# The first stage of a two-block layer kernel: order of the first loads, squares on two engines, and three of eight modulation blocks summed on VectorE

## The reference

```python
def rmsnorm(x, g):
    xf = x.astype(jnp.float32)
    xf = xf * lax.rsqrt(jnp.mean(xf * xf, axis=-1, keepdims=True) + EPS)
    return xf.astype(x.dtype) * g
...
    mod = c_act @ ada_w + ada_b                       # c_act = silu(c), one vector of 1024
    sh1, sc1, gt1, sh2, sc2, gt2 = [m[:, None, :] for m in jnp.split(mod, 6, axis=-1)]
    h = rmsnorm(x, mix_pre_g) * (1.0 + sc1) + sh1
    proj = h @ w_in
```

## Time and profile before

| | us |
|---|---|
| median of 3 runs (1496.1 to 1496.56) | 1496.12 |
| the profiled execution's own time | 1496.44 |
| its span in the trace | 1494.4 |
| PE busy / DVE / ACT / POOL in the span | 1482.8 / 783.5 / 528.4 / 952.2 |

### The profile page before, as it was taken

The page is one execution under the profiler, slowest core; times in us unless marked ns, Lnnn a source line. Parts: engine busy times, 40 slices in busy tenths (PEclk is TensorE's granted clock), DMA queues, the critical chain, the costliest instruction groups (busy, mean ns, idle before and its releaser), DMA issues.

```text
span 1494.4 us, 22386 instructions
## 1 busy us (share of the span) xinstructions
PE 1482.8 (99%) x7834; PEld 1213.3 (81%) x7834; DVE 783.5 (52%) x1088; ACT 528.4 (35%) x943; POOL 952.2 (64%) x945
## 2 busy tenths in 40 slices
PE   8999999999999999999999999999999999999998
PEld 6778877888788888888988888888888778787876
DVE  3556676576566657323755554400474572836533
ACT  4481641361262221112522222200342644645432
POOL 5456657665765789788277777798336564655543
PEclk9999999999999999999999999999999999999999
DMA  9244434533533344635022333344133222222231
GB/s 377 90 129 139 129 107 129 168 109 124 180 107 115 114 143 163 127 105 196 29 84 98 98 98 98 99 134 134 57 130 116 64 83 62 79 70 70 72 126 57
DMA packets 67981, 172.29 MB, mean 115 GB/s; under 512 B 7728, under 2 KB 24496, under 8 KB 66384
## 3 DMA queue, kind: packets, MB, share of 16 engines
q1 hardware_dynamic: 45504, 150.05, 30.9%
q10 hardware_dynamic: 22416, 21.44, 4.7%
HBM read 167.20 MB, written 4.27 MB: 115 GB/s over the span
## 4 chain that ended last, share of the span: by engine, by line
PE 97%; DVE 1%; ACT 1%; DMA 0%; issue 0%; SPq 0%; ACTq 0%; DVEq 0%
PE ps L604 17%; PE ps L606 17%; PE ps L607 17%; PE ps L621 6%; PE ps L623 6%; PE ps L622 6%; PE ps L972 4%; PE ps L970 4%; PE ps L971 4%; PE ps L872 1%; PE ps L1149 1%; PE ps L997 1%; PE ps L993 1%; PE ps L995 1%; PE ps L875 1%; PE ps L860 1%
## 5 line engine op out<-in xcount | busy, mean ns | idle before, releaser
L554 POOL TENSOR_SCALAR w_hi<-raw 128x512 fp32r<-128x512 f32 x388 | 262.4, 694 | 508.3 <-PE ps L607 242.6
L559 POOL TENSOR_TENSOR w_lo<-raw,w_hi 128x512 fp32r<-128x512 f32 x388 | 529.7, 1386 | 0.0
L604 PE MATMUL ps<-h_hi,w_hi 128*128 128x512 f32 x880 | 347.7, 395 | 0.2
L607 PE MATMUL ps<-h_hi,w_lo 128*128 128x512 f32 x880 | 342.9, 390 | 0.0
L606 PE MATMUL ps<-h_lo,w_hi 128*128 128x512 f32 x880 | 342.7, 389 | 0.0
L604 PEld LDWEIGHTS ps<-h_hi,w_hi 128*128 128x128 f32 x880 | 165.2, 188 | 39.2 <-issue 5.8
L607 PEld LDWEIGHTS ps<-h_hi,w_lo 128*128 128x128 f32 x880 | 165.2, 188 | 35.0
L606 PEld LDWEIGHTS ps<-h_lo,w_hi 128*128 128x128 f32 x880 | 165.3, 188 | 34.1 <-issue 1.0
L621 PE MATMUL ps<-h_hi,w_hi 128*128 128x512 f32 x352 | 142.0, 403 | 0.0
L623 PE MATMUL ps<-h_hi,w_lo 128*128 128x512 f32 x352 | 137.8, 391 | 0.0
L622 PE MATMUL ps<-h_lo,w_hi 128*128 128x512 f32 x352 | 137.4, 390 | 0.0
(11 more groups left out here) (431 smaller groups left out, 2841.0 us busy)
## 6 DMA issues: line engine op xcount, KB each, us to landing
raw<-stream SPq DMA_DIRECT2D x231, 512.0 KB, 3.3
ada_raw<-ada SPq DMA_DIRECT2D x64, 256.0 KB, 3.6
ada<-ada_first SPq DMA_DIRECT2D x8, 1024.0 KB, 14.7
abc<-acs_dram ACTq DMA_DIRECT2D x16, 512.0 KB, 7.1
raw<-stream SPq DMA_DIRECT2D x8, 256.0 KB, 12.0
xr<-x_classes ACTq DMA_DIRECT2D x1, 2048.0 KB, 10.6
x_dram<-xr ACTq DMA_DIRECT2D x1, 2048.0 KB, 8.2
x_res<-x_dram ACTq DMA_DIRECT2D x2, 1024.0 KB, 9.1
```

The source lines that it names most:

```text
L554: nc.gpsimd.tensor_scalar(hi[:, w], raw[:, raw_slot, w], 1.0, 1.0, ALU.mult, ALU.mult).then_inc(split_hi, 1)
L559: ins = nc.gpsimd.tensor_tensor(lo[:, w], raw[:, raw_slot, w], hi[:, w].bitcast(F32), ALU.subtract)
L604: nc.tensor.matmul(ps[:, bank], hi[:, w], x_hi[:, k0 + k], start=start and k == 0, stop=False)
L607: mm = nc.tensor.matmul(ps[:, bank], lo[:, w], x_hi[:, k0 + k], start=False, stop=stop and k == tiles - 1)
```

## The change

- The loads. All four tiles of x go first, in order, on SP's queue. `ada0[0]` comes ahead of the first halves of the weights; `ada0[2]` to `ada0[4]` come ahead of all second halves; the large table and `dt_raw` come last.
- The squares. ACT squares tiles 0 and 2, DVE tiles 1 and 3 (`tensor_tensor_reduce`). There is one root, one inversion of four columns, one diagonal matrix of 128 x 512, one spreading matmul of 512 columns, one copy. The four `keep_busy` matmuls that stood behind the spreading stand ahead of it, and two more are gone.
- The modulation. Blocks 0 to 3 and 7 are formed as before. Blocks 4, 5 and 6 are not formed on PE: DVE multiplies the eight slices of `ada0[b]` with the eight columns of silu(c) and sums them in `mod0_acc` (128 x 256), and `turn_mod` sums that over the partitions with a column of ones.
- `form_mod(2)` moves ahead of `first_tiles(0, (4,))`.

Core of the diff:

```diff
+MOD_ON_PE, MOD_ON_DVE = (0, 1, 2, 3, 7), (4, 5, 6)
...
-            sp.dma_start(x_tok[:, 0], arrays["x"][:, 0]).then_inc(x_in[0], 16)
-            sp.dma_start(x_tok[:, 2], arrays["x"][:, 2]).then_inc(x_in[2], 16)
+            for t in range(NT):
+                sp.dma_start(x_tok[:, t], arrays["x"][:, t]).then_inc(x_in[t], 16)
...
             def turn_mod(b):
-                pe.wait_ge(mod0_copied, b + 1)
-                if b == 0:
-                    pe.wait_ge(root_copied, 2)
+                if b in MOD_ON_DVE:
+                    n = MOD_ON_DVE.index(b)
+                    pe.wait_ge(mod0_parts, KT * (n + 1))
+                    rows, weight = mod0_acc[:, n], ones[:, 0:1]
                 else:
+                    n = MOD_ON_PE.index(b)
+                    pe.wait_ge(mod0_copied, n + 1)
+                    rows, weight = mod0_rows[:, n % 2], eps[:, 2:3]
+                if b:
                     pe.wait_ge(mod0_ready, 2 * b - 1)
...
-            pe.wait_ge(root_formed, 1)
-            for t in range(NT - 1):
-                mm = spread_root(t)
-            mm.then_inc(root_spread, 1)
-            keep_busy(2)
-            pe.wait_ge(root_formed, 2)
-            spread_root(NT - 1).then_inc(root_spread, 1)
             keep_busy(4)
+            pe.wait_ge(root_steps, 1)
+            nc.tensor.matmul(ps[:, 7], ones[:], root_diag[:].rearrange("p t q -> p (t q)"), start=True,
+                             stop=True).then_inc(root_steps, 1)
             form_mod(0)
             turn_late(5)
             turn_mod(0)
+            pe.wait_ge(root_steps, 3)
             keep_busy(3, 7)
...
             for k in range(2, KT - 1):
-                form_mod(k + 1)
+                if k + 1 in MOD_ON_PE:
+                    form_mod(k + 1)
                 first_tiles(k, (1, 2))
                 turn_mod(k + 1)
                 first_tiles(k, (3, 4))
...
+            def square_row(t):
+                dve.wait_ge(x_in[t], 16)
+                V.tensor_tensor_reduce(xn[:, 2 * t:2 * t + 2].rearrange("p b s -> p (b s)"), x_tok[:, t], x_tok[:, t],
+                                       1.0, 0.0, ALU.mult, ALU.add, small[:, 8 + t:9 + t]).then_inc(row_stats, 1)
...
+            def mod_pieces(b, ks):
+                n = MOD_ON_DVE.index(b)
+                dve.wait_ge(ada0_in[b], 16)
+                for k in ks:
+                    if k == 0:
+                        TS(mod0_acc[:, n], ada0[b][:, k], small[:, k:k + 1], None, ALU.mult).then_inc(mod0_parts, 1)
+                    else:
+                        dve.wait_ge(mod0_parts, KT * n + k)
+                        STT(mod0_acc[:, n], ada0[b][:, k], small[:, k:k + 1], mod0_acc[:, n], ALU.mult,
+                            ALU.add).then_inc(mod0_parts, 1)
+
+            head, tail = range(0, KT // 2), range(KT // 2, KT)
...
-            for b in range(2, DB):
-                first_h(b)
+            first_h(2)
+            mod_pieces(4, head)
+            first_h(3)
+            mod_pieces(4, tail)
+            mod_pieces(5, head)
+            first_h(4)
+            mod_pieces(5, tail)
+            mod_pieces(6, head)
+            first_h(5)
+            mod_pieces(6, tail)
+            first_h(6)
+            first_h(7)
```

More of the change, by code:

```diff
@@ L195, in build @@
         mod0_rows = g("mod0_rows", [P, 2, 2 * P])
+        mod0_acc = at("mod0_acc", FREE + 72 * KB, [P, len(MOD_ON_DVE), 2 * P])
         c_rep = g("c_rep", [P, KT, 32])
@@ L299, in build @@
         mod0_formed = sem("mod0_formed")
+        mod0_parts = sem("mod0_parts")
         mod0_copied = sem("mod0_copied")
@@ L487, in first_raw @@
                 sp.dma_start(raw[:, u % 4, w], arrays["stream"][u][:, w]).then_inc(landed, 16)
+            first_ada(0)
             first_raw(1, 0)
             first_raw(2, 0)
-            first_ada(0)
+            first_ada(1)
             for signal in start_at_one:
@@ L495, in _ @@
             first_raw(3, 0)
-            first_ada(1)
             first_raw(4, 0)
[L498 to L504, removed]
+            for b in (2, 3, 4):
+                first_ada(b)
+            first_raw(1, 1)
+            first_raw(2, 1)
             first_ada(5)
+            first_raw(3, 1)
+            first_raw(4, 1)
             first_ada(6)
@@ L508, in _ @@
             first_ada(7)
+            sp.dma_start(dt_raw[:], arrays["stream"][0, :, 0:KT * SSD_HEADS]).then_inc(dt_raw_in, 16)
+            sp.dma_start(tab[:, first_cols:NCOL], arrays["table"][:, first_cols:NCOL]).then_inc(tab_in, 16)
             def stream(u, slot):
@@ L729, in _ @@
             turn_late(6)
+            form_mod(2)
             first_tiles(0, (4,))
-            form_mod(2)
             first_tiles(1, (1,))
@@ L809, in conv @@
                     if first:
-                        free = {4: (mod0_copied, KT), 5: (conv_taps, 3)}[j]
+                        free = {4: (mod0_copied, len(MOD_ON_PE)), 5: (conv_taps, 3)}[j]
                     elif j >= 3:
@@ L1271, in _ @@
             A = nc.scalar.activation
-            for t in (1, 3):
-                act.dma_start(x_tok[:, t], arrays["x"][:, t]).then_inc(x_in[t], 16)
             act.wait_ge(ident_in, 16)
@@ L1790, in _ @@
             STT(small[:, 20:20 + DB], col("ada_b", 8, DB), 1.0, col("g_pre", 0, DB), ALU.add, ALU.mult).then_inc(setup, 1)
-            for first, last, stats in ((0, NT - 1, 4), (NT - 1, NT, 6)):
-                dve.wait_ge(row_stats, stats)
-                V.reciprocal(small[:, 16 + first:16 + last], small[:, 12 + first:12 + last]).then_inc(setup, 1)
-                dve.wait_ge(setup, 6 if first == 0 else 7)
-                TT(root_diag[:, first:last], ident.unsqueeze(1).broadcast_to([P, last - first, P]),
-                   small[:, 16 + first:16 + last].unsqueeze(2).broadcast_to([P, last - first, P]),
-                   ALU.mult).then_inc(root_formed, 1)
+            square_row(1)
+            square_row(3)
+            dve.wait_ge(row_stats, NT + 1)
+            V.reciprocal(small[:, 16:16 + NT], small[:, 12:12 + NT]).then_inc(setup, 1)
+            dve.wait_ge(setup, 6)
+            TT(root_diag[:], ident.unsqueeze(1).broadcast_to([P, NT, P]),
+               small[:, 16:16 + NT].unsqueeze(2).broadcast_to([P, NT, P]), ALU.mult).then_inc(root_steps, 1)
             def scale_x(b):
```

51 lines of the change are left out of this document (21 added, 30 removed).

## The result

The median of six runs is 1502.30 us (1501.75 to 1504.06), that of before beside it 1496.37 (six runs, 1496.10 to 1496.93). The ratio is 1.0042, with a 95% interval of 1.0031 to 1.0052: slower by 5.9 us (0.4%, and clear of the spread of the runs), where 1502.4 was forecast. The profiled execution took 1501.81.

What follows compares the result with a forecast made beforehand. PE, busy 99%, was taken as the bound, with first-stage losses passed on whole. DVE's pieces and POOL turns delay turn_mod(6) from 44.3 to 50.8, taken as 6.3: 1496.44 becomes 1502.7, less 0.3 is 1502.4; range 1497.5 to 1507.5.

Steps and rivals of the forecast that it cites:

- Part 1: Loads and roots at the start: turn_mod(0) near 14.7 in place of 17.15, a gain of about 2.4 us.
- one rate for the queue: Load queue: a steady 0.388 MB/us gives every landing of the new order, x tile 3 at 8.9.
- Part 2: Three forms off PE, 1.1 us each: PE cannot keep that; even with a free DVE a step gains 0.8.
- Part 3: Pieces on DVE, 0.45 and 0.03 hand-over each: DVE becomes the bound at k = 3, 4, 5; loss 6.5, taken as 6.3.
- The undisturbed step: DVE's steady step of tail pieces, head pieces, hf and h_lo: 5.0 us, against PE's 4.43.
- The turns: DVE and POOL alternate instructions, a turn costing nearly the sum; a piece costs 1.5 or 0.9, not 0.48.
- the first meeting: Between h_lo(2) and h_lo(3): six POOL instructions, 5.65 us, plus DVE's port time; h_lo(3) ends at 34.9.
- port time: DVE's own time added to POOL's 5.65 us before h_lo(3) ends: 4 x 0.25 + 0.4 + 0.55.
- The rival of longer pieces: DVE's pieces take 0.7, adding 0.22 x 20: 1507; chance 0.04, shared with longer squares.
- longer squares: DVE's square of an x tile, taken as 1.3, bound up to 2.5; chance 0.04, shared with longer pieces.
- a fallen clock: Rival: PE's clock falls, as PE sits still from about 30.4 to 34.9 and twice more for 2 us; chance 0.16.
- The rival without turns: Pieces of 256 slip between POOL's instructions at no cost; tail of 6 ends at 42.4: 1494.2; chance 0.14.

Runs made afterwards that it cites:

- E4: The changed kernel with constant keep_busy matmuls in PE's stops at k = 3, 4 and 5, to keep the clock up: 1501.77 us, ratio 1.0037.
- E12: E3 (24 pieces, running sums in PSUM) with 2 or 3 keep_busy matmul pairs in each of PE's stops of k = 3, 4 and 5: 1497.56 us.
- E1: The changed kernel with all eight modulation blocks formed on PE again, leaving the loads, squares and single root chain: 1494.34 us, ratio 0.9986.
- E5: The changed kernel with only block 6 on DVE, sum in PSUM, four pieces a step, ada0 loads reordered to suit: 1493.79 us, ratio 0.9983.
- E6: The changed kernel with only blocks 5 and 7 on DVE, sums in PSUM, four pieces a step, ada0 loads reordered: 1493.23 us, ratio 0.9978.
- E8: E6 with the running sums in SBUF, as in the changed kernel: 1496.28 us, ratio 0.9999.
- E11: E3 (running sums in PSUM) with the load order of E7 (second halves early): 1499.17 us, ratio 1.0016.
- E10: E7 (second halves early) with keep_busy matmuls on constants in PE's stops of k = 3, 4 and 5: 1499.27 us, ratio 1.0023.
- E3: The changed kernel with each block's running sum kept in PSUM, only the last piece writing to SBUF: 1498.92 us, ratio 1.0014.
- E7: The changed kernel with second halves of weight units 1 to 4 loaded earlier, ahead of later ada0 blocks: 1501.04 us, ratio 1.0030.

## Why the prediction was right

The mechanism was right: DVE became the bound of the stage, and the pieces took turns with POOL's splits. With the clock kept up in E4 and E12, the change can be taken apart by differences of medians:

| from | to | us |
|---|---|---|
| before, 1496.46 | E1, loads and roots | -2.1 |
| E1, 1494.34 | E12, 24 pieces without turns, eight in a step, three forms off PE | +3.2 |
| E12, 1497.56 | E4, the pieces take turns with POOL | +4.2 |
| E4, 1501.77 | the whole change, 1502.30 | +0.5 |

**Part 1.** Forecast 2.4, measured 2.1 in time (E1) and 1.75 at `turn_mod(0)` in the changed kernel's profile. `turn_mod(0)` stood at 15.40, not 14.7: x tile 3 was squared from 9.82 and not from 8.9, as my one rate for the queue was taken from transfers that land later and was too fast for its beginning, and the spreading took 1.12 in the place of 1.0. The square itself has 1.23 + 0.08 = 1.31, forecast 1.3. That `ada0[1]` might hold `form_mod(1)` came out at 0.16, a wait of its first weight load.

**Part 2.** A form off PE does not give its 1.1 us. The prediction allowed 0.8 with a free DVE; E5 and E6 show 0.55 for each.

**Part 3, the pieces.** A piece alone took 0.485 + 0.03, where I took 0.45 + 0.03 (bounds 0.40 to 0.50 for the first number); the first of eight 0.35 (0.34). The undisturbed step came out as forecast even so: from the head of block 6 at 44.81 to the end of its tail at 47.82 + 2.04 = 49.86 are 5.05 us, where the prediction has 5.0. The 5.31 of E12 is the step with sums in PSUM: its first piece takes 0.49 in the place of 0.35, and its rows stand a little further apart. So some 0.5 of the 3.2 us in the table (an estimate, 0.26 on each of two steps) belongs to that form of the sum, and the turns of the changed kernel may cost that much more than 4.2.

**The turns.** The chain came out place by place:

| end or start | forecast | measured |
|---|---|---|
| `h_lo(2)` ends | 27.3 | 27.7 |
| `h_lo(3)` ends | 34.9 | 34.4 |
| `turn_mod(4)` | 37.9 | 37.4 |
| `h_lo(4)` ends | 42.8 | 41.9 |
| `h_lo(5)` ends | 48.8 | 47.9 |
| `turn_mod(6)` | 50.8 | 49.9 |

At most 0.9 off. The term that was too large is the first meeting: from `h_lo(2)` to `h_lo(3)` 7.6 us forecast, 6.65 measured. The same six POOL instructions as forecast went by, but the first of them was under way at 27.27, before `h_lo(2)` ended, and the two engines overlap more than I took: from 27.27 to 33.91 the six take 6.64 us with DVE's between them. The prediction had added 1.95 us of DVE's own time (4 x 0.25 + 0.4 + 0.55, its "port time") to the 5.65 of POOL. No row or run shows such a time, nor the 0.25; what the runs showed in its place is about half of the 1.95, 6.65 us from `h_lo(2)` to `h_lo(3)` against the 5.65.

**Luck.** That the medians agree to 0.1 is in part luck. The sum started from the profiled execution, 1496.44 + 6.3 = 1502.7, and the profiled execution of the changed kernel took 1501.81, which is 5.4 more and not 6.3; at `turn_mod(6)` 6.5 was forecast and 5.61 measured. Then 0.3 was taken off for the median, which stands 0.5 above the profiled execution in the changed kernel. Within the sum errors of both signs met: the roots came 0.7 late and the fallen clock, put at nothing, cost up to 0.5, while the first meeting was 0.95 too long.

**The cause.** That the turns are a cause and not only go with the loss is shown twice: with the sums in PSUM 4.2 us go (E12 against E4), and with two blocks spread 3.05 (E6 against E8). The other form of the sum is not what gains: away from POOL a piece takes the same in both, 2.04 us for four in SBUF (the changed kernel at 47.82) and 1.54 for three in PSUM (E11 at 36.09), 0.51 each. That the late second halves make them meet is shown by E10 against E4 (2.5 us); that they act mostly in this way is what E11 suggests.

In the traces the turns go with where a piece's sum lies: a mean of 661 and 758 ns for the pieces with both inputs in SBUF (the changed kernel and E8), 488 for those with the sum in PSUM (E6), beside the same splits. The last piece of a block in E12, with one SBUF input and its output in SBUF, takes 0.48 beside POOL (at 34.00) and 0.48 with POOL idle (at 45.01).

The rival of longer pieces, 0.7 each, is out. No run shows a piece of that length away from POOL: four undisturbed pieces at 47.82 of the changed kernel take 2.04 together, 0.51 each. Its longer squares did not come either (1.31, above).

**The clock.** I gave 0.16 to a fallen clock and priced it at 3 us and more, under the condition that it is low from `turn_mod(6)` on; that price, the far end of the clock in the range, was my estimate, and no row of before shows a low clock in this stage. It did fall, to 0.50 in the first stop, and was back at 1.00 at 44.6, before that point. While it was low PE waited for DVE, and matmuls that come 0.43 apart and not 0.23 cost little where PE has slack: at most about 0.5 us (E4), which the spread of the runs does not tell from nothing. The condition itself is borne out by E3 and E7, where the clock was at 0.50 in the step of k = 6, which PE fills, and in place of the 3 us and more they showed 1.56 and 2.4 us in the profiled executions, 1.4 and 1.8 by the medians of E12 and E10, where the spread is as large. What decides in which step it falls was not settled; the stop ahead of it was 2.41 us in the changed kernel and 2.15 at the second fall of E7; ahead of E7's first none was over 1.24, and in E3 none over 1.09.

**The rival without turns** was priced at 1494.2. The nearest run, E12, has 1497.6, or some 1497.1 without what its form of the sum costs (an estimate). The rival had `h_lo(2)` at 26.3, where E12 has 27.4, and `h_lo(3)` at 30.5, where it has 32.5: `hf` and `h_lo` still take turns (1.27 and 0.98 between 30.2 and 32.5 of E12, beside POOL, in the place of 0.55 and 0.69 alone), and `hf` waits for `coef` until 30.23. And the second step meets the split of unit 5 (5.69).

**Expectations that missed.** E8's, because I looked at the number of instructions in a step and not at their length with turns; in E7's the clock, the stop at k = 3 and, by 0.04 us, the time; in E1's the place of `turn_mod(0)`; and E11's, where I had put part of what is left on the order of the loads.

## What to carry to other kernels

- Work that is taken off the full engine and given to one with idle time must be summed on the chain that it joins. Here DVE was idle for two thirds of the stage, in stretches of 2.82 us ahead of each `hf`; four pieces (2.0 us) fitted into one (E6), eight (4.0) did not.
- Before giving DVE more work beside POOL, look at where its running sum lies. The accumulation of 128 x 256 with its sum in PSUM kept its 0.49 us beside POOL's splits (E6, E12); the same one in SBUF took 0.66 in the changed kernel and 0.76 in E8, in the mean, against 0.51 alone.
- The effects of two edits need not add up: the loads that gained 2.1 us alone moved POOL's splits to where the pieces were, and the two together lost 3.4 us more than the sum of both. Look at what a moved transfer releases.

## What was unexpected in the hardware

- TensorE's granted clock fell to 0.50 in a single stop of 2.41 us (the changed kernel at 34.2), and in the profiled execution of E3 with no stop over 1.1 us. With it PE's matmuls came 0.43 us apart in the place of 0.23. With a few matmuls on constants in the stops its mean was 1.000 in all eleven runs of E12 and in eight of the eleven of E10. The fallen clock cost at most about 0.5 us where PE was waiting anyway, and 1.6 and 2.4 us in the profiled executions of E3 and E7, where it fell into a step that PE fills.
- A TENSOR_SCALAR with its output in SBUF takes turns with POOL (`hf` 0.55 alone, up to 1.48), while the first piece, a TENSOR_SCALAR of 128 x 256 from SBUF into PSUM, took 0.48 beside POOL (E12 at 27.34) and 0.49 alone (E11 at 35.56). With its output in SBUF it was 0.35 alone and 1.37 beside POOL: the faster form is the one that takes turns.
